# A decoder trunk on one core: where the first two weight units of the attention's output projection are split

## The reference

```python
def nsa_attention(h, w_qg, w_o, k_cmp, v_cmp, k_slc, v_slc, k_win, v_win):
    ...
    o = lax.map(query_block, jnp.arange(t // Q_BLOCK))
    o = jnp.moveaxis(o, 0, 1).reshape(b, t, NSA_Q_W).astype(h.dtype)
    return o @ w_o

    # in reference(), for layer 1:
    h = h + rms_norm(mix, mix_post_norm[i])
    h = channel_and_ple(h, i)
```

## Time and profile before

| quantity | value |
|---|---|
| median of 3 runs | 936.47 us (935.56 to 936.64) |
| the profiled execution | 937.43 us, its span 935.7 us |
| TensorE matmul busy | 893.5 us, 95% |
| VectorE busy | 584.6 us, 62% |
| ScalarE busy | 513.2 us, 55% |
| GpSimd busy | 55.5 us, 6% |
| DMA moved | 138.29 MB, mean 148 GB/s |

### The profile page before, as it was taken

How to read it: one execution, slowest core, us unless ns; L and a number is a source line. 1 busy time by engine, 2 the same in 40 slices (tenths; PEclk the granted TensorE clock), 3 DMA queues, 4 the chain that set the end, 5 groups by cost and what they waited for, 6 DMA issues and landing times.

```text
span 935.7 us, 14029 instructions
## 1 busy us (share of the span) xinstructions
PE 893.5 (95%) x5289; PEld 757.9 (81%) x5289; DVE 584.6 (62%) x964; ACT 513.2 (55%) x911; POOL 55.5 (6%) x82
## 2 busy tenths in 40 slices
PE   6989999999999999999999899998889999999998
PEld 6989988788888878888888789886567888888876
DVE  6876985767676575555544676777757555554465
ACT  6645655666766474444533559356856544443452
POOL 6000230302000000000000000000000000000000
PEclk9999999999999999999999999999999999999999
DMA  9941211111124657677555555420034565654552
GB/s 341 339 141 40 91 46 46 46 46 47 46 86 143 209 169 226 227 231 231 197 173 176 187 180 174 136 91 1 1 116 155 185 189 186 190 193 158 195 186 93
DMA packets 105900, 138.29 MB, mean 148 GB/s; under 512 B 4586, under 2 KB 76787, under 8 KB 105843
## 3 DMA queue, kind: packets, MB, share of 16 engines
q1 hardware_dynamic: 103650, 130.15, 42.8%
q0 software_dynamic: 2160, 7.36, 2.0%
q10 hardware_dynamic: 32, 0.01, 0.0%
HBM read 136.45 MB, written 1.05 MB: 147 GB/s over the span
## 4 chain that ended last, share of the span: by engine, by line
PE 77%; DVE 9%; ACT 9%; issue 2%; DMA 1%; SPq 0%; ACTq 0%; DVEq 0%
PE ps L528 16%; PE ps L530 16%; PE ps L529 16%; PE ps L507 5%; DVE w_lo L1607 4%; PE ps L512 4%; PE ps L514 4%; PE ps L513 4%; ACT w_hi L1138 3%; PE ps L739 2%; PE ps L759 2%; PE ps L1024 1%; DVE gdn L1674 1%; ACT qkvT L1541 1%; DMA w_raw<-in_ple_w_in 1%
## 5 line engine op out<-in xcount | busy, mean ns | idle before, releaser
L1607 DVE TENSOR_TENSOR w_lo<-w_raw,w_hi 128x2048 fp32r<-128x2048 f32 (+2 forms) x100 | 220.7, 2207 | 197.3 <-ACT w_hi L1138 197.3
L1138 ACT ACTIVATE w_hi<-w_raw 128x2048 fp32r<-128x2048 f32 (+2 forms) x100 | 184.5, 1845 | 184.0 <-PE ps L530 143.3
L528 PE MATMUL ps<-w_hi,x_hi 128*128 128x512 f32 x480 | 193.1, 402 | 5.6 <-DVE x_lo L1638 2.1
L530 PE MATMUL ps<-w_hi,x_lo 128*128 128x512 f32 x480 | 187.6, 391 | 0.0
L529 PE MATMUL ps<-w_lo,x_hi 128*128 128x512 f32 x480 | 187.1, 390 | 0.0
L528 PEld LDWEIGHTS ps<-w_hi,x_hi 128*128 128x128 f32 x480 | 90.2, 188 | 26.4 <-issue 4.8
L530 PEld LDWEIGHTS ps<-w_hi,x_lo 128*128 128x128 f32 x480 | 90.1, 188 | 19.5
L529 PEld LDWEIGHTS ps<-w_lo,x_hi 128*128 128x128 f32 x480 | 90.4, 188 | 16.7
L512 PE MATMUL ps<-x_hi,w_hi 128*128 128x256 f32 x320 | 91.4, 286 | 1.4 <-DVE w_lo L1607 1.0
L513 PE MATMUL ps<-x_lo,w_hi 128*128 128x256 f32 x320 | 90.5, 283 | 0.0
L514 PE MATMUL ps<-x_hi,w_lo 128*128 128x256 f32 x320 | 90.5, 283 | 0.0
(11 more groups left out here) (312 smaller groups left out, 1468.9 us busy)
## 6 DMA issues: line engine op xcount, KB each, us to landing
w_raw<-in_ffn_w_in SPq DMA_DIRECT2D x88, 512.0 KB, 4.5
w_raw<-in_ffn_w_out SPq DMA_DIRECT2D x40, 512.0 KB, 4.4
w_raw<-in_gdn_w_in SPq DMA_DIRECT2D x28, 512.0 KB, 4.6
gdn<-in_gdn_w_in SPq DMA_DIRECT2D x20, 512.0 KB, 7.6
w_raw<-in_gdn_w_out SPq DMA_DIRECT2D x16, 512.0 KB, 4.2
w_raw<-in_ple_w_gate SPq DMA_DIRECT2D x16, 512.0 KB, 4.6
w_raw<-in_kv_w SPq DMA_DIRECT2D x12, 512.0 KB, 4.0
qkvT<-in_cmp_w POOLq DMA_DIRECT2D x8, 512.0 KB, 5.0
```

The costliest lines, as they stand in the source:

```text
L528: mm(o, hi, w_h, start=first and kk == 0, stop=False, skip_group_check=True)
L530: return mm(o, lo, w_h, start=False, stop=end and kk == n - 1, skip_group_check=True)
L1138: A(whi[:, place(stage, q), c0:c0 + n], ring_raw(u) if stage == "qkv" else raw[:, q, 0:n], ACT.Copy).then_inc(S["hi_done"], 1)
L1607: V.tensor_tensor(wlo[:, s, c0:c0 + n], ring_raw(u) if stage == "qkv" else raw[:, q, 0:n], whi[:, s, c0:c0 + n], ALU.subtract).then_inc(S[ ...
```

## The change

ScalarE's quarters move to later rounds and behind the loop: round 5 does quarter 0, round 6 quarter 1, round 7 quarter 2, and quarters 3 to 7 follow the loop, ahead of out_hi(7). On VectorE round 6 does quarter 0, round 7 quarters 1 and 2, and 3 to 7 follow. VectorE now counts parts 0 to 2 in a new semaphore, `wq_lo`. For the first 512 columns TensorE waits ahead of each k for its quarter and then, as before, for `alo` (`wo_ready`). `post_stage` has a new argument, `by_quarter`, false by default: where it is true, the wait for the whole unit ahead of the first 512 columns' units is left out. No call in the kernel sets it.

```diff
-            def post_stage(name, ks, banks, xs, ready=None, after_first=None):
+            def post_stage(name, ks, banks, xs, ready=None, after_first=None, by_quarter=False):
 
                 per = len(ks)
                 for c in range(2):
                     for u in range(per):
-                        pe.wait_ge(S["lo_done"], U0[name] + c * per + u + 1)
+                        if c or not by_quarter:
+                            pe.wait_ge(S["lo_done"], U0[name] + c * per + u + 1)
                         k0 = sum(ks[:u])
...
             pe.wait_ge(S["p_act"], 16)
-            post_stage("wo", (4, 4), ((4, 5), (2, 3)), big_tok8, lambda k: pe.wait_ge(S["alo"], k + 1),
+            def wo_ready(k):
+
+                u, part = divmod(k, 4)
+                if part == 3:
+                    pe.wait_ge(S["lo_done"], U0["wo"] + u + 1)
+                else:
+                    pe.wait_ge(S["wq_lo"], 3 * u + part + 1)
+                pe.wait_ge(S["alo"], k + 1)
+            post_stage("wo", (4, 4), ((4, 5), (2, 3)), big_tok8, wo_ready,
                        lambda u: output(7) if u == 0 else None)
...
                 turned(p, 0)
-                for m in ((0,), (1,), (2,), (3,), (4,), (5,), (6, 7))[p - 1]:
+                for m in ((), (), (), (), (0,), (1,), (2,))[p - 1]:
                     wo_quarter(m)
                 turned(p, 1)
...
+            for m in range(3, 8):
+                wo_quarter(m)
             out_hi(7)
...
                 last = V.tensor_tensor(wlo[:, s, c4], raw[:, u, c4], whi[:, s, c4], ALU.subtract)
-                if part == 3:
-                    last.then_inc(S["lo_done"], 1)
+                last.then_inc(S["lo_done" if part == 3 else "wq_lo"], 1)
...
                 out_lo(p - 1)
-                if p >= 3:
-                    wo_quarter(p - 3)
-            for m in (5, 6, 7):
+                for m in {6: (0,), 7: (1, 2)}.get(p, ()):
+                    wo_quarter(m)
+            for m in range(3, 8):
                 wo_quarter(m)
             out_lo(7)
```

More of the change, by code:

```diff
@@ L245, in build @@
                      "gtri_done kq_ps dA_ps dA_ex dQ_ps dQ_ex qs_ps qs_sb a_sb qk_sb kt_ps ktok_sb vt_ps bv_sb w_init "
-                     "y_ps y_sb t_ps t_sb ap_sb ap_pool wp_sb zq_hi zq_lo hi_half wq_hi mk_dve p0_act mx0_dve z_ps w_upd u_ps vn_sb fv_sb s_ps s_sb ks_ps r1_sb o_ps o_sb o_sq on_dve on_root on_rec ot_sb "
+                     "y_ps y_sb t_ps t_sb ap_sb ap_pool wp_sb zq_hi zq_lo hi_half wq_hi wq_lo mk_dve p0_act mx0_dve z_ps w_upd u_ps vn_sb fv_sb s_ps s_sb ks_ps r1_sb o_ps o_sb o_sq on_dve on_root on_rec ot_sb "
                      "ot_ps ohi_done olo_done zs_sb "
```

## The result

The changed kernel takes 939.96 us (median of 9 runs, 938.08 to 943.21) against 936.47 us (9 runs, 935.56 to 937.54). The ratio is 1.0041 with a 95% interval of 1.0032 to 1.0049, that is 3.8 us more (3.0 to 4.6). The forecast was 938.6 us with a range up to 939.8. The medians themselves lie 3.5 us apart. The kernel is slower, as forecast, but by 1.7 us more than the sum of 2.1 us (by 1.4 us if the medians are taken).

A forecast was written before the change was run, and what follows sets the result against it. TensorE, busy 95% of the span, was taken to bound the kernel, so its few waits matter. A 2.1 us slip ahead of unit 0, all else 0, on the 936.47 us median gave 938.6 us, range 937.6 to 939.8.

The forecast's parts named there:

- the sum of 2.1 us: Whole kernel: the wait ahead of unit 0 costs 2.1 us, every other part of the change 0.
- The wait that stays: Ahead of unit 0 of the output projection: TensorE still waits for VectorE's quarter 3, now behind the rounds; cost 2.1 us.
- Nothing takes the slip back: Behind unit 0: output(7), out_hi(7), unit 2's split and its 0.46 us wait form one chain, so the 2.1 us remain.
- Quarters out of the rounds bring nothing: Attention rounds: without a quarter, ScalarE's and VectorE's waits grow by its step (0.52 and 0.60 us); gain 0.
- the waits cost nothing: Units 0 and 1: twelve more TensorE waits, long met in a full stream, cost 0; upper end 1.2 us.
- the loads are covered: Loads of units 2 and 3: issued later, yet landed before ScalarE asks; cost 0, with 4.6 us of cover.
- The clock: Rival, new wait ahead of unit 0: TensorE's clock falls to half, 5.5 us over unit 0's 24 matmuls, 944 us; chance 0.02.

The follow-up runs named there:

- the waits alone: Quarters stand as in the kernel before; of the change only the new semaphore, twelve added TensorE waits and the kept whole-unit wait remain: 937.37 us, ratio 0.9998.
- the second set: The changed kernel as it is, timed again beside the kernel with five added matmuls, against the kernel before: 939.98 us, ratio 1.0037.
- the longest slip here, 2.72 us: Changed kernel with quarter 4 ahead of quarter 3 behind the rounds on ScalarE and VectorE: 941.58 us, ratio 1.0055 to the kernel before.
- one of 1.28 us: Changed kernel with quarter 3 inside round 7 on both engines and quarter 1 inside round 6 on VectorE: 939.23 us, ratio 1.0022 to the kernel before.

## Why the prediction was right and where it failed

**The wait that stays: right.** The step that decides, that the call doesn't give `by_quarter` and TensorE waits for quarter 3, was read from the code, and giving the argument takes the whole loss away. Its size was 2.1 us; the traces show 2.12 and 2.11 us.

**Nothing takes the slip back: right.** The wait ahead of unit 2 is 0.46 us in both kernels.

**Quarters out of the rounds bring nothing, the waits cost nothing, the loads are covered: right.** With by_quarter the ratio is 0.9998; with the waits alone too. The rounds keep their length (6.83 us).

**The clock: the step that failed.** The prediction priced the clock's fall as a rival at 0.02 and put 0 in the sum. In the runs 12 of the changed kernel's 15 executions have a fall, and it cost 1.7 us on average; that alone puts the median beyond the range's 939.8 us. The step rested on the earlier trace rows: TensorE stood 3.64 us and the stretch behind had a granted clock of 1.00. I read the clock's column and not the durations beside it. The transposes of that stretch and those ahead of unit 0, both of 128 x 128 elements, in the kernel before (ns min/median/max):

```profile
L507 PE MATMUL ps<-ident,scr x16: 411/421/474, 8.7 to 12.0; 128*128 128x128 f32 x16
...
L507 PE MATMUL ps<-ident,qkvT x8: 272/273/328, 682.8 to 684.5; 128*128 128x128 f32 x8
```

The first take 421 ns each, the others 273; sixteen in 3.67 us are 0.23 us a piece, where six were followed by unit 0 after 0.76 us, or 0.13 us a piece. So behind that wait TensorE ran near half its pace although the column says 1.00, and the row can't speak against the rival. The trace of the changed kernel shows the same of the column, on the first matmuls of the product behind those transposes (TensorE's timeline, then the busy times by stretch):

```profile
13.81 0.41 PE L514 MATMUL ps<-x_hi,w_lo 128*128 128x256 f32 x1
14.03 0.41 PE L512 MATMUL ps<-x_hi,w_hi 128*128 128x256 f32 x1
...
14.65 0.28 PE L513 MATMUL ps<-x_lo,w_hi 128*128 128x256 f32 x1
...
12.00:14.20 2.20, 1.90 (x9) 1.52 (x8) 2.20 (x4) 2.20 (x6) 0.03 (x1) 1.00 1.08 376
```

Even read rightly the row is from the first microseconds, where next to nothing had run before (one matmul of 0.25 us), so it doesn't tell of a fall either. Behind the start the longest wait in the trace of before is 1.78 us, ahead of a matmul at 49.50, and the clock behind it is 1.00. The new one is longer, 1.87 us in the same count, and the clock should have been a term with a price and a real chance. The Trainium skill's rule (TensorE: Matmul & The Clock Gate, section What's actually happening), that an idle TensorE falls back to 1.2 GHz, was cited and outweighed by that row. One of the two traces of the changed kernel agrees with it, at 0.50 for the 5.7 us behind the wait; the other has the same wait of 1.87 us and stays at 1.00. The price of 5.5 us was an upper end over all 24 matmuls. In the profiled execution twelve steps were of 0.43 us, with a longer one at each end, and it was 2.8 us, and over the runs about 1.7 us (3.8 - 2.1). Only one of the nine runs had a mean clock of 1.0 over the span, and it took 938.08 us, 1.6 us over the median of before; in the second set two of six had it, 938.07 and 938.53 us, 1.3 and 1.8 us over. Within the 1 us by which single runs lie apart that is the time of the slip alone.

**The sum, corrected:** 2.1 us of slip and 1.7 us of clock on average, 940.3 us against a measured 939.96. The 1.7 us are what the measured difference leaves above the slip, so this sum is no test of them; that there is a clock's part of this kind is shown by the counts above and by the trace with 2.78 us.

Open stays what decides in one execution whether the clock falls: the longest slip here, 2.72 us, passed once in five without it, and one of 1.28 us had it four times in nine.

## What to carry to other kernels

When a change adds a flag that replaces a wait, look for the call that sets it: a wait by parts behind a wait for the whole is only a wait for the whole, and moving the parts later then costs the lateness of the last one (2.1 us here). A new wait of TensorE in the middle of dense work should be priced twice, its length and the chance that the matmuls behind run at half the clock; here the second part nearly doubled the first. And if an engine must wait, put useful work of its own there: with output(7) ahead of unit 0 the same wait cost nothing that could be measured.

## What was not expected of the hardware

The clock fell behind a slip of only 1.28 us, and not at once: the first matmuls behind the wait still ran at full pace, the next seven steps took 0.43 us. In the trace of the changed kernel it had come while TensorE stood. The granted clock as the profile lists it can read 1.00 where the matmuls themselves run near half pace, as at the start of both executions; durations of one form of instruction, at two places, tell. In the changed kernel's slowest execution the 5.7 us behind the wait ran at 0.50 in one piece. Five matmuls (1.1 us of work) in a wait of 2.1 us were enough: no fall in eleven executions, and the average loss down to the wait itself.
